# Forty modulation units of a four-part diffusion backbone, moved from TensorE side jobs to VectorE multiply-with-sum

## The reference, cut to what matters

```python
def rms_norm(x, g):
    y = xf * lax.rsqrt(jnp.mean(xf * xf, axis=-1, keepdims=True) + EPS)
    return (y * g.astype(jnp.float32)).astype(x.dtype)
def modulate(u, shift, scale):
    return u * (1 + scale) + shift
def channel_mixer(a, w1, w2):
    return jnp.square(jax.nn.relu(a @ w1)) @ w2
...
# per layer (what the kernel computes for the modulation):
#   mods = silu(c) @ w_ada + b_ada          (1024) @ (1024, 6*1024), for c and for c_ctx
#   -> shift, scale, gate of the mixer; shift, scale, gate of the feed-forward
#   u = modulate(rms_norm(h), shift, scale); y = mixer(u) or channel_mixer(u)
#   h = h + gate * rms_norm(y)
```

## Time and profile before

| | |
|---|---|
| time, median of 3 runs | 1923.66 us (1923.1 to 1924.69) |
| span of the profiled execution | 1923.4 us |
| TensorE busy | 1807.5 us (94%) |
| VectorE busy | 894.6 us (47%) |
| ScalarE busy | 691.6 us (36%) |
| GpSimd busy | 125.5 us (7%) |
| chain that ended last, TensorE's share | 87% |
| loads and stores on SP's queue | 160.37 MB |

### The profile page before, as it was taken

One profiled execution on the slowest core, in us unless ns is written; L12 is line 12 of the kernel. 1 busy time (PEld: TensorE's weight loads), 2 busy tenths in 40 slices (PEclk: granted clock), 3 DMA queues, 4 the chain that ended last, 5 costly groups with the idle time before them and its releaser, 6 DMA issues.

```text
span 1923.4 us, 28394 instructions
## 1 busy us (share of the span) xinstructions
PE 1807.5 (94%) x11476; PEld 1557.6 (81%) x11476; DVE 894.6 (47%) x1439; ACT 691.6 (36%) x1286; POOL 125.5 (7%) x300
## 2 busy tenths in 40 slices
PE   5899999999989799999999997889999969999997
PEld 3899666677789699899889975889877958888885
DVE  0453244446762633343343345861468354444445
ACT  3433344445544621122122225432467352232321
POOL 2200000000002100000000004000234000000000
PEclk9899999999999999999999998999999989999999
DMA  8111022255531111211111110120303113223231
GB/s 324 69 45 67 1 88 88 88 214 203 197 117 38 59 64 56 77 56 64 65 65 65 65 65 22 45 88 1 88 1 111 67 66 110 88 88 109 87 104 49
DMA packets 26552, 161.84 MB, mean 84 GB/s; under 512 B 3024, under 2 KB 5968, under 8 KB 8400
## 3 DMA queue, kind: packets, MB, share of 16 engines
q1 hardware_dynamic: 26448, 160.37, 23.4%
HBM read 156.17 MB, written 2.10 MB: 82 GB/s over the span
## 4 chain that ended last, share of the span: by engine, by line
PE 87%; DVE 4%; ACT 3%; issue 2%; POOL 2%; DMA 1%; SPq 0%; DVEq 0%; ACTq 0%; POOLq 0%
PE ps L918 21%; PE ps L700 14%; PE ps L702 13%; PE ps L701 13%; PE ps L751 6%; PE ps L782 4%; PE ps L721 3%; PE ps L856 2%; PE ps L771 2%; PE ps L634 2%; PE ps L831 1%; PE ps L728 1%; ACT junk L1198 1%; PE ps L713 1%; PE ps L819 1%
## 5 line engine op out<-in xcount | busy, mean ns | idle before, releaser
L700 PE MATMUL ps<-whi,uhi 128*128 128x512 f32 (+1 forms) x832 | 305.7, 367 | 4.3 <-DVE ulo L1652 3.2
L702 PE MATMUL ps<-whi,ulo 128*128 128x512 f32 (+1 forms) x832 | 304.1, 365 | 0.0
L701 PE MATMUL ps<-wlo,uhi 128*128 128x512 f32 (+1 forms) x832 | 304.1, 365 | 0.0
L1190 ACT ACTIVATE whi<-raw 128x2048 fp32r<-128x2048 f32 x89 | 169.8, 1908 | 296.5 <-PE ps L702 296.4
L1624 DVE TENSOR_TENSOR wlo<-raw,whi 128x2048 fp32r<-128x2048 f32 x89 | 204.0, 2292 | 124.7 <-ACT whi L1190 124.2
L700 PE MATMUL ps<-whi,ahi 128*128 128x256 f32 x752 | 219.4, 292 | 14.0 <-DVE wlo L1624 6.8
L701 PE MATMUL ps<-wlo,ahi 128*128 128x256 f32 x752 | 216.2, 287 | 0.0
L918 PE MATMUL ps<-ahi,whi 128*128 128x384 f32 (+1 forms) x720 | 215.3, 353 | 0.7 <-ACT relu L1473 0.6
L702 PE MATMUL ps<-whi,alo 128*128 128x256 f32 x752 | 216.0, 287 | 0.0
L918 PE MATMUL ps<-alo,whi 128*128 128x384 f32 (+1 forms) x720 | 215.2, 353 | 0.0
L918 PE MATMUL ps<-ahi,wlo 128*128 128x384 f32 (+1 forms) x720 | 215.2, 352 | 0.0
(11 more groups left out here) (207 smaller groups left out, 2571.7 us busy)
## 6 DMA issues: line engine op xcount, KB each, us to landing
raw<-in_w_ff SPq DMA_DIRECT2D x64, 1024.0 KB, 4.8
raw<-in_w_ada SPq DMA_DIRECT2D x42, 1024.0 KB, 4.8
raw<-in_w_in_odd SPq DMA_DIRECT2D x9, 1024.0 KB, 5.0
raw<-in_w_in_even SPq DMA_DIRECT2D x8, 1024.0 KB, 4.8
first_raw<-in_w_ada SPq DMA_DIRECT2D x6, 1024.0 KB, 15.8
h<-in_x SPq DMA_DIRECT2D x4, 1024.0 KB, 7.1
raw<-in_w_out_even SPq DMA_DIRECT2D x4, 1024.0 KB, 4.8
raw<-in_na_bias SPq DMA_DIRECT2D x4, 1024.0 KB, 5.9
```

Of the source, the lines that this page charges most:

```text
L700: pe.matmul(dst, lhs[0], rhs[0], start=first, stop=False)
L701: pe.matmul(dst, lhs[0], rhs[1], start=False, stop=False)
L702: return pe.matmul(dst, lhs[1], rhs[0], start=False, stop=last)
L1190: act.activation(whi[w % 2][:, :, :], raw[r % 2][:, :, :], ACT.Copy).then_inc(s_hi, 1)
```

## The change

The host no longer puts units 8 to 47 of `w_ada` in the layout of a matmul. It stores them transposed (`w_ada_t`): a partition holds two output columns' worth of 1024 inputs. SiLU of both conditioning vectors is computed on all partitions, as rows (`silu_rows`, 128 x 2 x 1024). A unit is then four VectorE instructions (two columns, two streams) of 128 x 1024 each, a multiply with a sum over the row that lands in one column of `mods`.

Twelve units run in the input projection of layer 0 (2, 2, 1, 1, 1, 1, 2, 2 by unit), 28 in the seven chunks of the feed-forward of layer 0, one in each weight unit: behind each hidden block two instructions, and in a down unit one ahead of each of the additions 2 to 5. Attention of layer 0 keeps only the `head` jobs. In the feed-forward the weights now all use `raw0`; the modulation units use `raw1`. The gate and scale columns that are needed later are formed later, in the feed-forward's tail for layer 1 and for layer 0's second gate.

```diff
+ADA_FIRST, ADA_EARLY = 8, 12
+EARLY_OF_UNIT = [2, 2, 1, 1, 1, 1, 2, 2]
...
-        elif unit < 48:
-            here.append(("ada", unit, 0))
...
+    return [[("head", h + 1, t)] if kind == "mla" and h + 1 < MLA_H and t < 4 else []
+            for kind, h, t in attention_steps()]
...
+    loads += [("ff", None)] * 2 + [("ff", None), ("adat", None)] * 28 + [("ff", None)] * 2
...
+            def ada_load(i, after_weights=False):
+                if after_weights:
+                    sp.wait_ge(s_lo, W_FF0 + 2)
+                else:
+                    sp.wait_ge(s_ada, i * 4)
+                src = w_ada_t[bass.ds(i, 1), :, :].rearrange("c p n -> p (c n)")
+                sp.dma_start(raw[1][:, :, :].rearrange("p k n -> p (k n)"), src).then_inc(s_raw[1], 16)
...
+                def quad(c, dyn, first=False):
+                    u, i = w0 + 2 + dyn, ADA_EARLY + dyn
+                    for j, (kind, chunk, half) in enumerate(((1, c, 0), (1, c, 1), (2, c - 1, 0), (2, c - 1, 1))):
+                        ff_load(0, kind, chunk, half, r0, w0 if first and j == 0 else u + j - 1)
+                        ada_load(i + j, first and j == 0)
...
+                ff_load(0, 2, 7, 0, r0, w0 + 29)
+                sp.wait_ge(s_ada, 4 * (ADA_EARLY + 28))
+                ff_load(0, 2, 7, 1, r0 + 1, None)
...
+            sp.dma_start(silu_rows[:, :, :].rearrange("p s n -> p (s n)"), crow.partition_broadcast(P)).then_inc(s_crow, 16)
...
+                if layer == 0:
+                    act.wait_ge(s_mod, 3)
                 for s in streams[layer]:
                     for half in range(2):
                         copy_group((f"gate{layer}1", s, half))
...
+            act.wait_ge(s_crow, 16)
+            act.activation(silu_exp[:, :, :], silu_rows[:, :, :], ACT.Exp, scale=-1.0).then_inc(s_srow, 1)
             input_projection(0, W_IN0, G_IN0)
...
+            def modulation_product(slot, piece, dst, scratch):
+                mt, s = divmod(piece, 2)
+                weights = raw[slot][:, :, :].rearrange("p k n -> p (k n)").rearrange("p (m n) -> p m n", m=2)
+                return dve.scalar_tensor_tensor(out=scratch[:, :], in0=weights[:, mt, :], scalar=1.0,
+                                                in1=silu_rows[:, s, :], op0=ALU.mult, op1=ALU.mult, accum_out=dst)
...
+                    if layer == 0:
+                        for i in range(sum(EARLY_OF_UNIT[:u]), sum(EARLY_OF_UNIT[:u + 1])):
+                            early_modulation(i)
...
                         if pos < 2:
                             for mt in range(2):
                                 hidden(f1b + 4 * c + 2 * pos + mt, f1d)
+                                if layer == 0:
+                                    piece(2 * mt)
+                                    piece(2 * mt + 1)
                         else:
-                            down(f2b + per * (c - 1) + nt * (pos - 2), pos - 2, f2d, first)
+                            down(f2b + per * (c - 1) + nt * (pos - 2), pos - 2, f2d, first,
+                                 piece if layer == 0 else None)
...
+                if layer == 0:
+                    dve.wait_ge(s_mcopy, 3)
+                    modulation(40, 96)
+                    link(scale_columns(1, 0))
+                    link(scale_columns(1, 1))
+                    link(gate_columns(1, 0))
+                    link(gate_columns(1, 1))
+                    gate_columns(0, 1).then_inc(s_mod, 1)
+                    dve.wait_ge(s_mod, 3)
...
+            dve.wait_ge(s_srow, 1)
+            link(dve.tensor_scalar(silu_exp[:, :, :], silu_exp[:, :, :], 1.0, None, ALU.add))
+            link(dve.reciprocal(silu_exp[:, :, :], silu_exp[:, :, :]))
+            link(dve.tensor_tensor(silu_rows[:, :, :], silu_rows[:, :, :], silu_exp[:, :, :], ALU.mult))
             input_projection(0, W_IN0)
```

More of the change, by code:

```diff
@@ L64, in side_jobs, with build @@
 def side_jobs():
[L67 to L71, removed]
-        elif unit < 48:
-            here.append(("ada", unit, 0))
[L74 to L81, removed]
+    return [[("head", h + 1, t)] if kind == "mla" and h + 1 < MLA_H and t < 4 else []
+            for kind, h, t in attention_steps()]
+def build(nc, x, ctx, cols, rows, consts, tables, na_bias, w_ada, w_ada_t, crow, w_ff1, w_ff2, w_in_even,
           w_out_even, w_uq, w_ukv, w_in_odd, w_out_odd, out):
@@ L388, in build @@
         raw_of_ada = [r for r, l in enumerate(loads) if l[0] == "ada"]
+        raw_of_adat = [r for r, l in enumerate(loads) if l[0] == "adat"]
         R_OUT0 = raw_of_unit[W_OUT0]
@@ L1481, in step @@
                     q = w0 + 2 + 4 * (c - 1)
-                    f1d, f2d, rawd = i * (4 * n), i * (per * n), i * (32 * n)
+                    f1d, f2d, rawd = i * (4 * n), i * (per * n), i * ((64 if layer == 0 else 32) * n)
                     for pos in range(4):
@@ L1997, in hidden, with modulation_step, down @@
                                       uhi[:, m % 8, 0:width].bitcast(F32), ALU.subtract).then_inc(s_ulo, 1)
-                def down(g, half, dyn, first=False):
+                def modulation_step(i, piece, dyn, dst):
+                    if piece == 0:
+                        dve.wait_ge(s_raw[1], 16 * (raw_of_adat[ADA_EARLY + i] // 2 - 2) + dyn * 64)
+                    dve.wait_ge(s_ada, 4 * (ADA_EARLY + i) + piece + dyn * 16)
+                    modulation_product(1, piece, dst, ada_junk).then_inc(s_ada, 1)
+                def down(g, half, dyn, first=False, between=None):
                     for t in range(nt):
+                        if between is not None and 1 <= t < 5:
+                            between(t - 1)
                         dve.wait_ge(s_f2, g + t + 1 + dyn)
@@ L2106, in later_modulation @@
             def later_modulation():
-                dve.wait_ge(s_jobf, job_count)
-                modulation(16, 96)
-                for layer, sub in ((0, 1), (1, 0), (1, 1)):
-                    link(scale_columns(layer, sub))
-                for layer in range(2):
-                    for sub in range(2):
-                        last = gate_columns(layer, sub)
-                last.then_inc(s_mod, 1)
+                dve.wait_ge(s_ada, 4 * ADA_EARLY)
+                modulation(16, 40)
+                link(scale_columns(0, 1))
+                gate_columns(0, 0).then_inc(s_mod, 1)
                 dve.wait_ge(s_mod, 2)
@@ L2193 @@
     consts = np.concatenate([np.eye(P), np.ones((P, P)), selects], axis=1).astype(np.float32)
+    ada_rows = np.stack([a["w_ada"][u // 24][:, UW * (u % 24):UW * (u % 24) + UW].T.reshape(2, P, D).transpose(1, 0, 2)
+                         .reshape(P, 2 * D) for u in range(ADA_FIRST, 48)])
     arrays = {
```

65 lines of the change are left out of this document (55 added, 10 removed).

## The result

The changed kernel takes 2007.95 us (median of four runs, 2004.56 to 2009.74) beside 1924.18 us of the kernel before on the same chip (1923.1 to 1925.41): 4.3% slower, ratio 1.0431, 95% interval 1.0419 to 1.0444. The prediction said 2029 us, with 1945 to 2095 for 8 in 10. The profiled execution has a span of 2002.6 us, 79.2 more than that of before.

A forecast was written before the change was run, and what follows sets the result against it. TensorE, busy 1807.5 of 1923.4 us, was taken as the bound. 1923.4 - 57 (attention) + 13 (start) + 145 (feed-forward) + 5 (tail) = 2029 us, chance 0.67; 8 in 10 for 1945 to 2095.

The forecast's parts named there:

- The mechanism: Layer 0's feed-forward: paired loads wait for the previous unit's products, making a serial loop; chunk 87.0 us instead of 66.0.
- Feed-forward: Layer 0's feed-forward: first chunk loses 18.8 us, six more 21.0 each, 145 us in sum.
- The product: One VectorE multiply-with-sum over 1024, price unknown: taken as 1.4 us, bounds 1.22 and 1.6.
- both unknowns high: Feed-forward with second load landing at 9.7 us and product at 1.6: chunk loses 31 us, sum 210.
- Rival 2: VectorE's products run at half pace, 2.4 us each; 2142 us in all; chance 0.11.
- Rival 1: Feed-forward loads hardly hinder each other, products cost at most 1.28 us; chunk loses 9 to 10, total 1949; chance 0.12.
- Is TensorE ever the later one in this loop?: Feed-forward: no; TensorE's last hidden block is done at +14.5 us, VectorE comes at +17.5, so its pauses cost nothing more.
- Rival 3: Feed-forward loop is not serial, weights land while VectorE works, nothing lost there; 1884 us; chance 0.06.
- Attention: Attention of layer 0: removing 40 jobs of 1.43 us TensorE work gains 57 us, between 52 and 61.
- the cover: Attention: in a step without a job VectorE still has 0.9 us to spare, so TensorE stays covered.
- The start: Input projection: a reciprocal of 13.4 us delays unit 1; TensorE loses 11.5 plus 1.6 slow clock, together 13 us.
- The tail: Feed-forward's end: eight small instructions and the last unit's late load cost TensorE 5 us (3 to 9).

The follow-up runs named there:

- e1: The changed kernel with the weight load of unit k+1 ahead of the modulation load of unit k on SP's queue in layer 0's feed-forward: 1890.79 us.
- e6: The changed kernel with the feed-forward's 28 modulation loads cut to 16 numbers per partition, 8 KB instead of 1 MB: 1976.28 us.
- e5: The changed kernel with all 112 products in layer 0's feed-forward over 16 numbers instead of 1024: 1956.18 us.
- e8: The changed kernel with only the 56 products of the feed-forward's down units 16 wide: 1999.69 us.
- e9: The changed kernel with only the 56 products of the feed-forward's hidden units 16 wide: 1963.01 us.
- e4: The kernel before without its forty side jobs in attention, their modulation columns set to zero: 1877.51 us.
- e3: The changed kernel with the weight load ahead of the modulation load and the row form of SiLU computed earlier: 1879.06 us.
- e7: The changed kernel with the 128x2048 reciprocal replaced by a multiply with a constant: 1995.90 us.

## Why the prediction was right, and where it was off

**The mechanism was right.** Sign, place and cause were as predicted: loads issued in pairs behind the fourth product, VectorE on `whi`, ScalarE on the load, TensorE idle for 11.4 us at the fifth down tile. e1 shows it by changing nothing but the order of the loads. Two of the signs that the prediction named did not come true as stated: the chunk took 81.8 us and not 85 to 89, and the fifth tile of the second down unit waits 0.3 us and not some 3.

**Feed-forward: 145 predicted, 113.8 measured; this term alone was mis-sized by more than the total miss.** It was 31 us too high, and attention's gain 7 us too high; the two errors have opposite signs in the sum, so the total was off by 27 us of span only. That part is luck. The first chunk lost 18.4 us by TensorE's rows (predicted 18.8), the other six 15.9 each, not 21.0. Per round: hidden 22.0 and 22.3 from one `split_lo` to the next (predicted 23.2), down 18.7 and 18.8 (predicted 20.3). The wait for the pair of loads was near (9.4 us from the last product to `split_lo`, predicted 7.7 + 1.94). What was too dear is the work: the product was taken at 1.4 us and steps at the next start after 1.14 to 1.27; and I added rows' durations, where the next instruction starts before the last one's has run out: `split_lo` 2.29 long and 2.21 apart, additions 0.68 long and 0.60 apart. In a serial chain the distance from start to start is what counts. A down unit's work is then 7.05 us and not 8.4. The range's upper end was also summed too low: with both unknowns high the prediction's own terms give 21.0 + 8.0 + 3.2 = 32.2 us a chunk (it says 31) and about 220 us in all (it says 210).

**The product.** 1.22 us and a read of the sum of 0.08:

```profile
L1891 DVE SCALAR_TENSOR_TENSOR ada_junk<-raw,silu_rows 128x1024 bf16<-128x1024 f32 x160 | 195.5, 1222 | 3.7 <-DMA raw<-in_w_ada_t 1.1
```

Rival 2 (half pace, 2142 us) is out. The Trainium skill ("Vector Engine (DVE) Microarchitecture Reference", section 7) says that this form, with two sources in SBUF that are not bf16, runs at half throughput; the trace has it at the pace of the plain product of that size (1.222 us), so here the measurement decides against the page.

**The second load.** Rival 1 needed loads that hardly hinder each other. They do hinder each other: 6.6 us against 4.8, and e6, with the modulation load nearly gone, shortened three rounds by 1.6 to 1.9. But that gave back 32 us of the 114, where the order of e1 gave back all of them (from the first square to the last addition in the loop it takes 478.9 us, as before).

**"Is TensorE ever the later one in this loop?"** The prediction said no, and that its pauses and its slow clock cost nothing more. In the changed kernel this held by 0.13 us only in the round read above, where the prediction had 3 us to spare. The margin was worked out for a round of 23.2 us and not for four rounds in a row; e5, e6, e8 and e9 show the chain through TensorE that lies beside VectorE's at the same length. Behind TensorE's pause the granted clock was at its 1.2 GHz level, 0.50:

```profile
862.39:866.00 3.61, 3.61 (x9) 2.84 (x10) 3.61 (x7) 0.00 (x0) 0.00 (x0) 0.50 0.00 0
```

**Rival 3 did not happen in the changed kernel, but a swap on SP's queue brings it about.** It was priced at 1884 us for a loop that is not serial; e1, where the loop is not serial, has 1890.79. The largest term between them is attention's 7 us.

**Attention: 57 predicted, 50.2 measured.** Two steps of this term failed. A job was worth 1.38 us of TensorE's work and not 1.43, which is 2 us of the 7. And the prediction let the new small waits cancel against the old load wait; they did not: e4, with the same 50.0, has 3.2 + 3.0 us of them against 0.4 + 1.2 before, and 5.2 us more idle time in all. The step read for the cover, with VectorE idle for 0.9 us, was one kind of step of several.

**The start: 13 predicted, 11.8 measured.** The reciprocal took 12.95 us (predicted 13.4), and TensorE waits behind it (VectorE's row, then TensorE's):

```profile
72.04 12.95 DVE L2182 RECIPROCAL silu_exp<-silu_exp 128x2048 f32<-128x2048 f32 x1
```

```profile
89.70 0.58 PE L742 MATMUL ps<-whi,ahi 128*128 128x256 f32 x1 [8.39 <-DVE wlo L1671]
```

12.95 us are 6.3 ns a number, the slope that two small rows gave (0.095 us for 15 numbers; the prediction wrote 6.5). `split_lo` was done at 89.6 and not 91.6; the slow clock behind the pause cost about 2.6 us (an estimate: 0.58 granted over the next 6.3 us) and not 1.6. The Trainium skill ("VectorE: DVE Perf Modes", section on the first, fixed hardware budget) speaks of a repeat count of eight; as eight cycles of its 0.96 GHz a number that would be 17 us, an estimate from that page, and the trace does not bear it out.

**The tail: 5 predicted, 4.5 measured.** e1 and e3 keep most of it: from the first square of the feed-forward to the first addition of the last down unit they take 490.0 and 489.9 us, before 486.8. There the loop loses nothing, so these 3 us are the tail's. In e1's trace the diagonals start 2.16 us behind the start of the last addition in the loop, before 0.60: 1.6 us are the small instructions (seven, not eight). The other 1.6 lie behind the diagonals; their cause was not tried.

## What to carry to other kernels

When work is added to an engine with time to spare, look first at the queue that feeds it: a load that waits for the new work holds back every load behind it, so put the load that the bottleneck needs ahead of the one that waits (that alone turned 4.3% slower into 1.8% faster here). In a chain, add distances from start to start, not durations. Before expecting a cut to pay in full, look for a second chain of the same length: the same cut was worth 8 us in one kind of unit and 45 in the other. And when a pause goes, count the slow clock behind it too: of the 114 us, 21 were TensorE's own work stretched.

## What the runs showed of the hardware

- A multiply-with-sum of two float32 rows of 1024 on 128 partitions takes 1.22 us on VectorE, as long as the product without the sum; reading the sum takes 0.08 us more.
- A reciprocal on VectorE takes 12.95 us for 128x2048, 5.7 times a float32 product of that size (2.29 us).
- Of two 1 MB loads issued 0.6 to 1.0 us apart, the second lands 6.6 us after its own issue (median; 6.2 to 7.8), a single one 4.8; with the first cut to 8 KB it is 4.8 again.
- An addition of a constant (changed kernel) and a multiply with one (e7) on 128x2048 float32 take 1.23 us each, about half of the product of two such tensors (2.29 us).
